# A gated-DeltaNet layer: the 32x32 diagonal blocks of each triangular inverse are solved on GpSimd, one block a partition

## The reference, cut to what matters

```
lower = where(strict, beta[..., :, None] * kk * decay, 0.0)
rhs = concatenate([v * beta[..., None], k * (beta * exp(g_cum))[..., None]], axis=-1)
sol = triangular_solve(lower, rhs, left_side=True, lower=True, unit_diagonal=True)
...
u = u_i - w_i @ state          # for each chunk, in order
o = qd_i @ state + qk_i @ u
state = state * gl_i + kd_i^T @ u
```

## Time and profile before

| | |
|---|---|
| median of 3 runs | 1942.49 us (1941.36 to 1943.52) |
| profiled execution, its own time | 1941.34 us |
| its span, first to last instruction | 1939.7 us |
| mean granted TensorE clock | 0.975 |
| busy: PE, DVE, ACT, POOL | 95%, 48%, 27%, 10% |
| instructions on PE | 9059 |

### The profile page before, as it was taken

The page is one execution under the profiler, slowest core; times in us unless marked ns, Lnnn a source line. Parts: engine busy times, 40 slices in busy tenths (PEclk is TensorE's granted clock), DMA queues, the critical chain, the costliest instruction groups (busy, mean ns, idle before and its releaser), DMA issues.

```text
span 1939.7 us, 24525 instructions
## 1 busy us (share of the span) xinstructions
PE 1846.8 (95%) x9059; PEld 1496.7 (77%) x9059; DVE 937.8 (48%) x1361; ACT 517.8 (27%) x933; POOL 187.4 (10%) x202
## 2 busy tenths in 40 slices
PE   6999898998999999999989997999999999999997
PEld 5878687787777777777768876888888888888876
DVE  6665656756644535445465326333343333333336
ACT  3322232322344444444331112211111112111111
POOL 1200214224120211102000000000000000000000
PEclk7899999999999999999999997999999999999998
DMA  7733243443611222221054520210221022102002
GB/s 241 211 117 105 95 139 114 130 139 110 157 42 52 87 65 74 72 88 50 30 202 150 174 66 27 72 44 22 66 65 43 22 65 62 41 27 65 22 1 98
DMA packets 187467, 167.22 MB, mean 86 GB/s; under 512 B 5593, under 2 KB 168538, under 8 KB 187418
## 3 DMA queue, kind: packets, MB, share of 16 engines
q1 hardware_dynamic: 179786, 139.03, 24.7%
q0 software_dynamic: 7632, 27.53, 3.6%
HBM read 129.05 MB, written 37.49 MB: 86 GB/s over the span
## 4 chain that ended last, share of the span: by engine, by line
PE 82%; DVE 8%; issue 4%; ACT 3%; DMA 3%; SPq 1%; DVEq 0%; ACTq 0%; POOLq 0%
PE pm L716 33%; PE ps L716 18%; PE pm L1016 12%; PE aT L885 3%; PE aS L908 3%; PE gps L857 3%; PE gps L860 2%; PE aT L896 1%; PE gps L862 1%; DMA qkvb_d<-est 1%; ACT w_hi L1063 1%; PE gps L779 1%; DVE est L1380 1%; PE gps L832 1%; DVE w_lo L1301 1%
## 5 line engine op out<-in xcount | busy, mean ns | idle before, releaser
L1301 DVE TENSOR_TENSOR w_lo<-w_raw,w_hi 128x1024 fp32r<-128x1024 f32 x105 | 133.7, 1274 | 529.7 <-ACT w_hi L1063 518.7
L716 PE MATMUL pm<-act_hi,w_hi 128*128 128x512 f32 x832 | 257.4, 391 | 4.0 <-DVE act_lo L1350 4.0
L716 PE MATMUL pm<-act_lo,w_hi 128*128 128x512 f32 x832 | 257.4, 391 | 0.0
L716 PE MATMUL pm<-act_hi,w_lo 128*128 128x512 f32 x832 | 256.5, 390 | 0.0
L716 PE MATMUL ps<-act_hi,w_hi 128*128 128x512 f32 x720 | 251.4, 430 | 2.9 <-DVE est L1385 2.9
L1063 ACT ACTIVATE w_hi<-w_raw 128x1024 fp32r<-128x1024 f32 x105 | 110.8, 1056 | 498.2 <-PE pm L716 492.4
L716 PE MATMUL ps<-act_lo,w_hi 128*128 128x512 f32 x720 | 227.3, 397 | 0.0
L716 PE MATMUL ps<-act_hi,w_lo 128*128 128x512 f32 x720 | 225.4, 394 | 0.0
L716 PEld LDWEIGHTS pm<-act_hi,w_hi 128*128 128x128 f32 x832 | 156.5, 188 | 36.8 <-issue 4.2
L716 PEld LDWEIGHTS pm<-act_lo,w_hi 128*128 128x128 f32 x832 | 156.7, 188 | 33.0
L716 PEld LDWEIGHTS pm<-act_hi,w_lo 128*128 128x128 f32 x832 | 156.6, 188 | 33.1
(11 more groups left out here) (257 smaller groups left out, 2401.4 us busy)
## 6 DMA issues: line engine op xcount, KB each, us to landing
w_raw<-in_w_in_dram SPq DMA_DIRECT2D x45, 512.0 KB, 5.8
w_raw<-in_w_ffn_in_dram SPq DMA_DIRECT2D x44, 512.0 KB, 3.7
a_raw<-in_w_ada_dram SPq DMA_DIRECT2D x32, 512.0 KB, 3.9
f_raw<-in_w_ffn_out_dram SPq DMA_DIRECT2D x22, 512.0 KB, 4.1
adab<-in_w_ada_dram SPq DMA_DIRECT2D x8, 1024.0 KB, 7.8
qkvb_d<-est POOLq DMA_DIRECT2D x12, 512.0 KB, 2.9
qkva_d<-est POOLq DMA_DIRECT2D x12, 512.0 KB, 6.2
ast<-qkva_d SPq DMA_DIRECT2D x24, 256.0 KB, 6.2
```

The source lines that it names most:

```text
L716: ins = pe.matmul(dst[:, cols], wt[:, ds % 2, k, :], at[:, cols], start=(first and n == 0), stop=(last and n == 2))
L1301: dve.tensor_tensor(w_lo[:, ds % 2], w_raw[:, ds % NR], w_hi[:, ds % 2].bitcast(F32), ALU.subtract)\
```

## The change

The inverse of the four 32x32 diagonal blocks of each head (16 blocks in all) no longer comes from TensorE's first five levels. SP writes the blocks of `Lt` to DRAM (`low_d`) and loads them to `LB`, each block to 8 partitions, each of which works out 4 of the 32 rows of the block's inverse. POOL does forward elimination there: 31 columns, each a multiply and a subtract (`eliminate`, placed at slots 11 and 14). SP writes the result `Xi` to DRAM and loads it onto the diagonal of `Um`. TensorE then has 8 steps at slots 24 to 31: Q_T0 transposes `Um`, Q_Y5 and Q_U6 make the inverse of the 64x64 blocks (`Uf`), and Q_Z, Q_W, Q_V apply the 128x128 inverse to `Xm` without forming it; Q_AY and Q_KY follow. The steps at the start also change places: Q_D goes to slot 1, Q_TK, Q_TQ, Q_TO to 2, 3, 4, Q_GK and Q_GQ to 6 and 7, Q_QS and Q_KS to 8 and 9, Q_TV to 10. DVE's norms are now computed at Q_TQ.

```diff
-        Q_TK, Q_TQ, Q_TO, Q_D, Q_QS, Q_KS, Q_GK, Q_GQ, Q_TV, Q_T0 = range(10)
-        NQ = 30
-        GSLOT = list(range(1, 31))
+        (Q_D, Q_TK, Q_TQ, Q_TO, Q_GK, Q_GQ, Q_QS, Q_KS, Q_TV,
+         Q_T0, Q_Y5, Q_U6, Q_Z, Q_W, Q_V, Q_AY, Q_KY) = range(17)
+        NQ = 17
+        GSLOT = [1, 2, 3, 4, 6, 7, 8, 9, 10, 24, 25, 26, 27, 28, 29, 30, 31]
...
+            def low_blocks(t):
...
+                for d in range(P // BLK):
+                    sp.dma_start(diagonal_d(low_d, d), diagonal(Lt, d)).then_inc(low_stored, 16)
+                landed = sp.to_reg(t * 64 + 64)
+                sp.wait_ge(xT_stored, 16)
+                sp.wait_ge(low_stored, landed)
+                sp.dma_start(LB[:, :, :].rearrange("p i j -> p (i j)"),
+                             low_d.rearrange("b i j -> b (i j)").unsqueeze(1).broadcast_to([NBLK, CG, BLK * BLK]))\
+                    .then_inc(low_in, 16)
+            def inverse_blocks(t):
...
+                sp.wait_ge(xi_ready, solved)
+                sp.dma_start(inv_d.rearrange("b (g c) r -> (b g) (c r)", g=CG),
+                             Xi[:, :, :].rearrange("p c r -> p (c r)")).then_inc(inv_stored, 16)
...
+                sp.wait_ge(inv_stored, landed)
+                for d in range(P // BLK):
+                    sp.dma_start(diagonal(Um, d), diagonal_d(inv_d, d)).then_inc(inv_in, 16)
...
+                if s == 11:
+                    pool.wait_ge(low_in, t * 16 + 16)
+                    eliminate(range(0, 10))
+                if s == 14:
+                    eliminate(range(10, BLK - 1))
...
+            def eliminate(columns):
+                for j in columns:
+                    n = BLK - 1 - j
+                    x = X0 if j == 0 else Xi
+                    ch.link(pool.tensor_tensor(pr[:, :, 0:n], bc_mid(LB[:, j, j + 1:], CPG), x[:, :, j:j + 1]
+                                               .broadcast_to([P, CPG, n]), ALU.mult))
+                    ins = pool.tensor_tensor(Xi[:, :, j + 1:], x[:, :, j + 1:], pr[:, :, 0:n], ALU.subtract)
+                    if j < BLK - 2:
+                        ch.link(ins)
+                    else:
+                        ins.then_inc(xi_ready, 1)
...
                 elif q == Q_T0:
-                    pe.wait_ge(u0_ready, t + 1)
+                    pe.wait_ge(inv_in, t * 64 + 64)
```

More of the change, by code:

```diff
@@ L417, in _, with load_ada_columns @@
             A_COLS = (C_QA, C_KA, C_VA, C_Z)
             B_COLS = (C_GA, C_GA + P, C_GB, C_GB + P)
+            def load_ada_columns(i, a):
+                sp.wait_ge(asc_ready, i * ADA_PER + a + 1)
+                sp.dma_start(a_raw[:, a % 2], w_ada_v[:, :, bass.ds(i * (ADA_PER * P) + (2 * D + a * P), P)])\
+                    .then_inc(a_in[a % 2], 16)
             def projection_a(i, last):
[L422 to L442, removed]
@@ L588, in _ @@
                     .then_inc(row7_ready, 1)
-            for s in range(LEVELS):
-                b = 1 << s
-                odd = lvl[:, s, :].rearrange("p (n two b) -> p n two b", two=2, b=b)[:, :, 1, :]
+            for n, b in enumerate((BLK, 2 * BLK)):
+                odd = lvl[:, n, :].rearrange("p (n two b) -> p n two b", two=2, b=b)[:, :, 1, :]
                 nb = P // (2 * b)
@@ L839, in gdn_step @@
                             ins.then_inc(gst_free, 1)
-                elif q == Q_Y:
+                elif q == Q_Y5:
+                    pe.wait_ge(ct_ready, t * 2 + 1)
+                    for h in range(B_H):
+                        ins = pe.matmul(hd(gps, h), Ct[:, 0, h * P:(h + 1) * P], hd(Tm, h), start=True, stop=True)
+                elif q == Q_U6:
+                    for h in range(B_H):
+                        ins = pe.matmul(hd(gps, h), hd(Tm, h), hd(Um, h), start=True, stop=True)
+                elif q == Q_Z:
                     pe.wait_ge(xm_ready, t + 1)
                     for h in range(B_H):
-                        ins = pe.matmul(hd(gps, h), hd(Um, h), hd(Xm, h), start=True, stop=True)
+                        ins = pe.matmul(hd(gps, h), hd(Uf, h), hd(Xm, h), start=True, stop=True)
+                elif q == Q_W:
+                    pe.wait_ge(ct_ready, t * 2 + 2)
+                    for h in range(B_H):
+                        ins = pe.matmul(hd(gps, h), Ct[:, 1, h * P:(h + 1) * P], hd(zt, h), start=True, stop=True)
+                elif q == Q_V:
+                    for h in range(B_H):
+                        ins = pe.matmul(hd(gps, h), hd(Uf, h), hd(Tm, h), start=True, stop=True)
                 elif q == Q_AY:
@@ L850, in gdn_step @@
                         ins = pe.matmul(hd(gps, h), hd(kd, h), hd(ym, h), start=True, stop=True)
[L851 to L864, removed]
                 ins.then_inc(gdn_mm, 1)
@@ L1128, in gdn_read_act @@
             def gdn_read_act(t, q, order=None):
[L1130 to L1138, removed]
+                dst = {Q_TK: kd, Q_TV: vn, Q_T0: Tm, Q_Y5: Tm, Q_Z: zt, Q_W: Tm}.get(q)
                 if dst is not None:
@@ L1145, in gdn_read_act @@
                     act.activation(ybst[:, :], gps[:, :], ACT.Copy, scale=ngh[:, :]).then_inc(gdn_read, 1)
[L1146 to L1150, removed]
+                if q == Q_TK:
                     act.wait_ge(gdn_read, t * NQ + q + 1 + LEAD)
@@ L1154, in gdn_read_act @@
                             .then_inc(ssk_ready, 1)
+                if q == Q_TQ:
+                    act.wait_ge(gdn_mm, t * NQ + q + 1 + LEAD)
+                    act.wait_ge(ssk_ready, t * 4 + 4)
+                    for h in range(B_H):
+                        ins = act.activation(hd(junk, h), hd(gps, h), ACT.Square, accum_out=sskq[:, 4 + h:5 + h])
+                    ins.then_inc(gdn_read, 1)
                 if q == Q_D:
```

150 lines of the change are left out of this document (97 added, 53 removed).

## The result

The changed kernel takes 2000.67 us (median of 4 runs, 1999.02 to 2003.54), the kernel before 1941.92 (4 runs, 1940.15 to 1943.52): a ratio of 1.0304, 95% interval 1.0286 to 1.0322. It is 59 us slower where +25 was forecast: slower, as forecast, but by more than twice as much. The time lies inside the wide range (1921 to 2005) and above the forecast's own (1945 to 1990).

The account below looks back on a forecast made before the run. TensorE was taken to bound the kernel before; after, a chain through DVE, DRAM and POOL bounds A. A +38.0, B -33.6, seams +20.4 give +24.8 us, 1967; own range 1945 to 1990, wide range 1921 to 2005.

Parts of the forecast that it names:

- The clock: TensorE's lower clock after its waits at Q_T0 and Q_D: 2 us an A iteration, 1.2 for a B seam.
- Back: Trip of the inverse from the end of the elimination through DRAM to Q_T0, in A: 6.3 us.
- the gain of a B iteration: 9.4 us off TensorE's list less 1.0 for the scores' chain: 8.4 us, four times, -33.6.
- The two late things: TensorE waits at Q_D for `gm` (8 us in A, 5.6 at B seams) and at Q_T0 in A (15 us).
- E: Length of POOL's elimination, 62 operations: 24 us undisturbed, 28 in A with DVE's disturbance; bounds 14 and 40.
- the trip out: In A, `Lt` stored to DRAM and loaded to `LB`: ready at 13.0, landed at 20.6 us after Q_D.
- Rival 3: DRAM trips are longer because blocks move in 128-byte runs: 2 us more each trip, +16, 1983; chance 0.07.
- The seam: Q_D's wait for `gm` at three seams between B iterations: 5.6 us each plus 1.2 of clock, together +20.4.
- Rival 1: The elimination is quick, 0.22 us an operation, E = 17: -21, 1922; chance 0.26.
- Rival 2: Small POOL operations cost 0.55 us, E = 38: +40 on the forecast, 2007; chance 0.10.
- Rival 4: TensorE stays the bound and nothing is late: -75, 1867; chance 0.02.
- Rival 5: In B, POOL's operations take the memory path from DVE and the scores' chain falls behind: +24, 1991; chance 0.05.

Follow-up runs that it names:

- 76 filling matmuls: Changed kernel with 76 matmuls that nobody reads issued on TensorE before Q_T0 in the A iterations: 1994.2 us, ratio 1.0273 to the kernel before.
- the run with late stores: Changed kernel with POOL's two 512 KB stores and SP's next conditioning load held until the `Um` loads land, in A: 1990.1 us, ratio 1.0249 to the kernel before.
- the hybrid with `gm` early: A iterations as in the kernel before, B iterations as in the changed kernel with `gm` made early in B: 1918.72 us, ratio 0.9885 to the kernel before.

## Why the prediction was right and wrong

**What failed.** Four terms of the sum were too favourable, none of them the elimination: "The clock" (2 us an A iteration, measured 4.8), the trips ("Back" 6.3, measured 8.1, and `LB` 1.0 later), the gain of a B iteration (8.4, measured 6.6), and Q_D's wait in front of the first chunk (nothing, measured 10.3). The chain itself was right.

**Right: the mechanism.** The two late things stood at their places, TensorE waited for no `Um` in B, and the elimination took 29.4 us with its store where 28.6 was forecast. Piece by piece: POOL's operations go from 0.45 us (124 elements) to 0.20 (4), with 0.07 to 0.09 between them. Without store and stretching, the first B iteration has 26.7 - 1.3 - 1.6 = 23.8 us (610.88 to 637.58), the second A iteration 29.4 - 1.3 - 4.3 = 23.8, where I had E = 24 from the row of 64 elements. DVE stretches five operations of that A iteration to between 1.10 and 1.34 us, 4.3 us in all, for the 3.8 forecast. The store costs 1.3 with the wait that it brings, for 0.6. That Q_T0 to the next Q_D came out at 27.2 us at full clock, for 27.1, bears out the links over DVE. The Trainium skill ("GPSIMD Engine Reference", Elementwise — side-by-side cycle accounting) had led to 26 us undisturbed; the trace of after does not agree, it shows 2 us less.

**Wrong: "The clock", 2 us an A iteration.** It is 4.8 by the slots. Behind the wait at Q_D the first two slots take 4.4 and 2.2 us instead of 2.3 and 1.8; behind the wait at Q_T0 they take 3.5 and 2.9 instead of 1.8 and 2.3, and with 76 filling matmuls that whole stage is back at 27.2. The half behind Q_T0 is shown by that run. The half behind Q_D is only read from the slots: k's transposes start 2.1 us late and `Lt` is 2.6 late, but no run takes away this lower clock alone. The prediction gave no working for its 2 us; it is about the price of one wait, and there are two on the chain. 2.8 us too little, four times: 11 us.

**Wrong: "Back", 6.3 us, and the trip out.** I took one price for a small DMA, with nothing for the POOL stores that move in the same slots. The way back is 8.1 us, and 4.9 without the large transfers: the price I took was 1.4 us too high for a quiet trip, and that luck hid part of the 3.2 us that the large transfers cost. `LB` is there 1.0 us later than forecast (it lands in 4.3 us, for 3.5); why, no run shows. 2.8 us, four times: 11 us. Rival 3 had this cost at 4 us an iteration but blamed the 128-byte runs; the run with late stores shows the same runs landing in 1.6 to 1.9 us when nothing large is beside them.

**Wrong in size: B.** In the hybrid with `gm` early, the shorter list gives 7.3 us in one B iteration and 5.8 in the next, where I had 8.4. In the first, TensorE's busy time falls by 8.7 us (111.89 to 103.22) for the 9.4 forecast, and longer waits for the scores' chain (the longest 1.85 us, for `Pm`) take 1.3 for 1.0. In the second the same wait is followed by the lower clock, which takes 1.5 more. The seam costs 5.7 on average for the 6.8 forecast, but otherwise divided: 3.3 of wait, where the `ya_d` store lands in 2.9 us, and 2.4 of lower clock (PE busy for 106.4 us instead of 104.0 with as many instructions), for 5.6 and 1.2.

**The sum.** At the first B iteration +38 was forecast and +64.5 measured. That is four times the 16.1 us of the second A iteration, for four times 9.5, but it comes so by a swap. From slot 1 to slot 1 the four A iterations last 91.3, 91.2, 91.8 and 89.1 us where they lasted 79.3, 75.3, 75.1 and 81.4: 52 more, and hardly a seam in the fourth, where both kernels wait for `modT`. The other 12 are Q_D's wait in front of the first chunk: `gm` was ready at 217.7 before the change too, but slot 1 stood at 207.3 and had no need of it. The prediction had no term for it. First the two rows before, then the one after:

```profile
207.32 0.60 PE L822 MATMUL gps<-ident,gst 128*128 128x128 f32 x4
...
216.53 1.17 POOL L635 TENSOR_TENSOR gm<-incl,g 128x512 f32<-128x512 f32 x1
```
```profile
219.05 2.07 PE L898 MATMUL gps<-gm,after 128*128 128x512 f32 x2 [10.27 <-POOL gm L701]
```

From the first B iteration on it is -6.8 instead of -13.2: 4 x 1.8 less gained by the shorter list, 3 x 1.1 less lost at the seams, and 2.5 more lost, which lie in the first B iteration (114.8 us) and the last, which no run took apart. 26.5 + 6.4 = 33 us is the miss in the profiled executions. Rivals 1, 2 and 4 are out: the elimination is neither quick nor slow, and TensorE does not bound the A iterations. Rival 5, B suffering from POOL's use of the memory path, can be in the 1.3 us of longer waits at most.

What stays open: how much shorter the trip out would be with SP's loads moved away from it, and whether a hybrid with the A iterations' elimination made 11 us long would beat the one that was run.

## What to carry to other kernels

Work handed to an idle engine is free only as long as the whole loop through it, with both trips, is shorter than what TensorE has to do meanwhile: here 64.5 us of TensorE's work in an A iteration stood against a chain of 91, while the same change in the B iterations alone, with 104 us of TensorE's work to cover it, gained 0.3%, and 1.2% with `gm` early. Before moving a step to the first slot, follow what made its operand: the cover in front of Q_D had cost nothing, and making `gm` early, once it was lost, gave back 33 us. Price a wait of TensorE with the two slots behind it, at the lower clock, and a small DMA by the large ones that the same slots issue.

## What the runs showed of the hardware that was not expected

- Of four 16 KB loads, which all land in 1.6 to 1.9 us with nothing large beside them, the slowest takes 5.0 to 5.2 us in every A iteration where two 512 KB stores and a 512 KB load are issued within about 2 us of them.
- The length of a wait alone does not tell whether TensorE's lower clock follows. At Q_T0 waits of 2.93 us and more were followed by it (transposes 0.91 to 1.12 us instead of 0.66), one of 2.33 too (1.03), one of 2.36 only from the product step behind (1.91 instead of 1.05), and waits of 0.17 to 0.34 not at all. But in the hybrid with `gm` early the same wait of 1.84 to 1.85 us for `Pm` was followed by a granted clock of 1.00 over the next 11 us in one B iteration (from 641.9) and 0.84 in the next (from 748.7):

```profile
641.90:652.90 11.00, 11.00 (x57) 7.62 (x58) 5.04 (x12) 2.99 (x9) 3.49 (x3) 1.00 0.22 54
748.70:759.70 11.00, 10.98 (x47) 7.49 (x47) 4.39 (x10) 2.55 (x7) 3.50 (x3) 0.84 0.09 21
```

- GpSimd operations of 0.25 to 0.40 us beside a DVE operation on two SBUF inputs take 1.10 to 1.34 us, 0.8 to 0.9 more each, where the 512-element `gm` goes from 1.05 to 2.00: a short one is hit as hard as a long one.
